# Experts stage of a mixture-of-experts block: a fifth product bank, silu on ScalarE, a quarter of the low parts on GpSimd, and an earlier turn of the gated rows

## The chip, the cores and the metric

The kernel runs on one core of one Trainium2 chip. A core has TensorE (PE: matmuls and the weight loads ahead of them), VectorE (DVE), ScalarE (ACT), GpSimd (POOL) and SyncE (SP), which run their own instruction streams and meet through semaphores, and 16 DMA engines. SBUF is the on-chip memory of 128 partitions; PSUM has eight banks into which PE writes its products. The metric is the device time of one launch in microseconds (us), lower is better.

## What is computed

Two blocks in a row on 2048 tokens of width 1024, all float32: a hybrid mixer block, then (after an embedding norm that puts 16 meta tokens in front) attention of two kinds and a mixture of 32 experts with the four best of them for each token. The change is in the experts. Their part of the reference:

```python
def _clamped_swiglu(hgu):
    x_glu = jnp.minimum(hgu[..., ::2], SWIGLU_LIMIT)
    x_lin = jnp.clip(hgu[..., 1::2], -SWIGLU_LIMIT, SWIGLU_LIMIT)
    return x_glu * jax.nn.sigmoid(SWIGLU_ALPHA * x_glu) * (x_lin + 1.0)
...
    xs = h[tok]
    hgu = lax.ragged_dot(xs, w_gate_up, group_sizes) + b_gate_up[e_sorted]
    act = _clamped_swiglu(hgu)
    out = lax.ragged_dot(act, w_down, group_sizes) + b_down[e_sorted]
```

SWIGLU_LIMIT is 7, SWIGLU_ALPHA 1.702, w_gate_up is 32 x 1024 x 2048 and w_down 32 x 1024 x 1024.

## The kernel before

Seven stages follow each other: mixer, join, project, attend, route, experts, combine. The route stage sorts the rows by expert and writes tables (`R.tab`, and `tabd` with the row numbers). The experts stage, from about 3101 to 6178 us, is a loop over 32 groups; a group is an expert with up to 512 rows, that is r = 1 to 4 row blocks of 128. Each engine runs its own copy of that loop (experts_sync, experts_pool, experts_pe, experts_act, experts_dve) with its own order written out by hand; blocks b >= r are skipped by branches on values read from the table. Nothing else sets the order.

A group has six phases c, one for each slab of 512 columns: c = 0 to 3 are gate and up, c = 4 and 5 are down. For each slab SP loads 2 MB into `raw[c % 2]` (two phases ahead). To keep float32 precision each product is made of three: weights and rows are split into a high part (fp32r) and a low part. ACT casts the slab's four pieces of 128x1024 to `wh` (`high`, L2354), DVE subtracts them from raw into `wl` (`lows`, L2407), in phase c for the slab of c+1. When all four low pieces are done, DVE gives `raw` back to SP (`raw_free`). PE (`product`, L2311) then makes, for each row block b, 24 matmuls of 128x512 into one PSUM bank, `product_bank(c, b) = (b + 2c) % 4`; it takes `g_free` of the bank first. For b = 0 it takes `w_full` before k = 0, 2, 4, 6, one for each low piece.

DVE empties a bank in one of two ways. `gated` (c < 4, L2441 to L2447) adds the bias (`e_tt`), clamps gate (`e_gg`) and up (`e_uu`), waits for ACT's sigmoid (`e_sg`, L2386) and multiplies them into `e_act`. `outcome` (c = 4, 5, L2453) adds the bias into `e_Y`, which ACT stores to `yd`.

In between come transposes of PE, which are called turns here. `acts(c-1, b)` (L2294) turns the gated rows of the last phase into bank 6 or 7 (`TA`), ACT takes their high part (L2340), DVE the low part (`e_aTl`, L2407). `rows(b)` (L2286) turns the next group's gathered rows in banks 4 and 5 (`TX`), a half in each, in c = 4 at k = 4; blocks that the present group hasn't got are turned in c = 5 at k = 6. `between` says where in a product each stands: `acts` after two of eight k (after four for b = 0, except in c = 4). POOL's loop loads the row numbers (`e_idx`) of the group and gathers its row blocks into the two buffers of `hx` (L2269), each by an indirect DMA whose landing it waits for. `settle` is a 1x1 memset with a wait for it, `link` a wait for the instruction itself, `take` a wait on a semaphore that is then counted down.

The trace puts every wait of the stage down to L2204, the line of `take`.

## Time and profile before

| | us |
|---|---|
| median of three runs | 6391.53 (6390.81 to 6391.83) |
| profiled execution, whole | 6390.21 |
| its span | 6389.1 |
| experts stage in it | 3101 to 6178 |

| engine | busy us | share of the span |
|---|---|---|
| PE matmul | 5677.8 | 89% |
| PE weight load (beside matmuls) | 4489.7 | 70% |
| DVE | 3814.2 | 60% |
| ACT | 2232.1 | 35% |
| POOL | 749.0 | 12% |

Busy times are of the whole span. The record of a matmul lasts longer than the distance to the next one, since they are pipelined; distances are read from starts. An idle time in square brackets stands before the instruction that ended it, with what released it. A window is named by its two ends in us from the span's start. The DMA queue of SP lands a slab of 2 MB in 8.0 to 8.4 us in the middle.

### The profile page before, as it was taken

To read this page: it belongs to the slowest core of one execution; us is meant where nothing else is said; L and a number is where in the kernel's file an instruction comes from. 1 tells how busy PE (TensorE), PEld (TensorE's weight loads), DVE (VectorE), ACT (ScalarE), POOL (GpSimd) and SP (SyncE) were. 2 spreads that over 40 slices of the span, in tenths; PEclk is the share of its full clock that TensorE was granted. 3 is DMA by queue.
4 is the path that set the end of the run, shared out by engine and by line. 5 is a ranking of instruction groups with operands and counts; after the bars stand their busy time and mean duration, and the time that the engine had idled before them with its cause. 6 is when DMAs were issued, how large, how long until landed. Compare 5 with 4: busy or idle time off the path is not lost. (4 is left out here: it accounts for less than half of the span.)

```text
span 6389.1 us, 82690 instructions
## 1 busy us (share of the span) xinstructions
PE 5677.8 (89%) x26393; PEld 4489.7 (70%) x26394; DVE 3814.2 (60%) x7593; ACT 2232.1 (35%) x4436; POOL 749.0 (12%) x566
## 2 busy tenths in 40 slices
PE   8999896997999999979699999999998999988960
PEld 7777675775777777757577777777776877766740
DVE  6676574223555666657556556556566555666658
ACT  3444412333333344433233233333344232444421
POOL 1111053221000000025200000000000000000016
PEclk9999998998999999989799999999999999999985
DMA  3333333446210010033244444435455343565557
GB/s 134 116 115 104 112 125 111 126 126 212 85 44 35 28 41 22 9 113 105 86 167 160 147 159 171 158 135 200 175 206 208 127 154 142 201 224 217 204 191 259
DMA packets 278153, 871.47 MB, mean 136 GB/s; under 512 B 22304, under 2 KB 167312, under 8 KB 235664
## 3 DMA queue, kind: packets, MB, share of 16 engines
q1 hardware_dynamic: 228256, 744.21, 33.0%
q0 software_dynamic: 24576, 77.83, 3.8%
q10 hardware_dynamic: 24944, 45.37, 1.9%
q8 instruction: 119, 1.95, 0.1%
q14 instruction: 258, 2.11, 0.1%
HBM read 723.15 MB, written 144.18 MB: 136 GB/s over the span
## 5 line engine op out<-in xcount | busy, mean ns | idle before, releaser
L2407 DVE TENSOR_TENSOR e_wl<-r_raw,e_wh 128x1024 fp32r<-128x1024 f32 x772 | 908.7, 1221 | 344.6 <-DVEq L2204 344.6
L2311 PE MATMUL ps<-e_wh,e_hTh 128*128 128x512 f32 x2496 | 1026.0, 411 | 67.8 <-PEq L2204 67.8
L2311 PE MATMUL ps<-e_wh,e_hTl 128*128 128x512 f32 x2496 | 1002.7, 402 | 0.0
L2311 PE MATMUL ps<-e_wl,e_hTh 128*128 128x512 f32 x2496 | 1001.5, 401 | 0.0
L2354 ACT CAST e_wh<-r_raw 128x1024 fp32r<-128x1024 f32 x772 | 769.2, 1049 | 193.7 <-ACTq L2204 186.5
L2311 PEld LDWEIGHTS ps<-e_wh,e_hTh 128*128 128x128 f32 x2496 | 479.9, 192 | 187.7 <-issue 84.5
L2311 PE MATMUL ps<-e_wh,e_aTh 128*128 128x512 f32 x1248 | 513.6, 412 | 58.6 <-PEq L2204 58.6
L2311 PEld LDWEIGHTS ps<-e_wh,e_hTl 128*128 128x128 f32 x2496 | 478.4, 192 | 115.8
L2311 PEld LDWEIGHTS ps<-e_wl,e_hTh 128*128 128x128 f32 x2496 | 480.2, 192 | 104.3
L2386 ACT ACTIVATE e_sg<-e_gg 128x256 f32<-128x256 f32 x312 | 130.7, 419 | 1205.4 <-ACTq L2204 1205.4
L1614 PE MATMUL ps<-a_PT,a_V 128*128 128x512 f32 (+1 forms) x1088 | 548.9, 596 | 0.7 <-ACT a_oT L1670 0.7
L1683 DVE TENSOR_REDUCE a_sc<-ps 128x1 f32<-128x416 f32 (+1 forms) x640 | 365.2, 588 | 257.4 <-PE ps L1592 257.4
L2311 PE MATMUL ps<-e_wh,e_aTl 128*128 128x512 f32 x1248 | 496.2, 398 | 0.0
L2311 PE MATMUL ps<-e_wl,e_aTh 128*128 128x512 f32 x1248 | 495.7, 397 | 0.0
L1592 PE MATMUL ps<-a_K,a_Q 128*128 128x416 f32 (+1 forms) x1920 | 456.3, 367 | 21.3 <-DMA a_KR<-kTd 18.2
L1592 PEld LDWEIGHTS ps<-a_K,a_Q 128*128 128x128 f32 x1920 | 356.4, 189 | 77.4 <-issue 70.7
L2441 DVE TENSOR_TENSOR e_tt<-ps,e_bg 128x512 f32<-128x512 f32 x312 | 215.4, 690 | 310.1 <-DVEq L2204 309.5
L2269 POOL DMA_INDIRECT e_hx<-h1d,e_idx x78 | 89.4, 1146 | 2493.2 <-POOLq L2204 2301.9
L1600 PEld LDWEIGHTS ps<-ident,a_P 128*128 128x128 f32 (+1 forms) x2176 | 258.5, 138 | 170.5 <-issue 131.2
L1663 ACT ACTIVATE a_P<-ps,a_sc 128x416 f32<-128x416 f32 (+1 forms) x640 | 378.1, 606 | 0.0
L380 PE MATMUL ps<-m_xh,m_wh 128*128 128x512 f32 x896 | 353.8, 395 | 5.3 <-DVE m_wl L665 5.3
L1697 DVE COPY a_PT<-ps 128x512 f32<-128x512 f32 x384 | 265.2, 692 | 152.1 <-PE ps L1600 152.1
(358 smaller groups left out, 9547.3 us busy)
## 6 DMA issues: line engine op xcount, KB each, us to landing
r_raw<-in_wgu SPq DMA_DIRECT2D x130, 2048.0 KB, 8.4
r_raw<-in_wdn SPq DMA_DIRECT2D x64, 2048.0 KB, 8.0
m_raw<-in_w SPq DMA_DIRECT2D x56, 1024.0 KB, 4.9
yd<-e_Y ACTq DMA_DIRECT2D x156, 256.0 KB, 7.6
e_bg<-in_bgu SPq DMA_DIRECT2D x32, 1024.0 KB, 10.8
qTd<-p_qt SPq DMA_DIRECT2D x32, 640.0 KB, 5.9
yd<-a_zt SPq DMA_DIRECT2D x32, 512.0 KB, 6.7
e_bd<-in_bdn SPq DMA_DIRECT2D x32, 512.0 KB, 8.9
```

Source lines behind the costliest of these rows:

```text
L380: t = pe.matmul(p[:, :], x[:, w, i, j * 128:(j + 1) * 128], y[:, c % 2, i, :], start=(n == 0), stop=(n == 23))
L1592: t = pe.matmul(p[:, 0:w], x, y, start=(n == 0), stop=(n == len(todo) - 1))
L1600: t = pe.transpose(p[0:n, k * 128:(k + 1) * 128], P.P[:, m % 2, c * 512 + k * 128:c * 512 + k * 128 + n], ident[:])
L1614: t = pe.matmul(ps[b][:, :], P.V[0:r, n % 2, j, :], P.PT[0:r, G % 2, j, :], start=(j == 0), stop=(j == NT - 1))
L1663: act.activation(P.P[:, m % 2, lo:lo + w], p[:, 0:w], ACT.Exp, bias=P.sc[:, m % 2, 6:7], scale=scale, accum_out=P.sc[:, m % 2, 8 + c:9 + c ...
L1683: dve.tensor_reduce(z[:, c:c + 1], p[:, 0:SCW[c][1]], AX, ALU.max).then_inc(*v.step("max", m, c))
L1697: dve.tensor_copy(P.PT[:, G % 2, 4 * c:4 * c + 4, q], p[:, :].rearrange("p (k q) -> p k q", k=4)).then_inc(*v.step("t", n, c))
L2311: t = pe.matmul(E.G[g][:, :], x[:, b, k, :], y[:, c % 2, k, :], start=(n == 0), stop=(n == 23))
L2354: act.copy(E.wh[:, n % 2, 2 * i:2 * i + 2, :].rearrange("p k n -> p (k n)"), E.raw[:, n % 2, 2 * i:2 * i + 2, :].rearrange("p k n -> p (k ...
L2386: act.activation(E.sg[:], E.gg[:], ACT.Sigmoid, scale=1.702).then_inc(E.sig, 1)
L2407: return dve.tensor_tensor(lo, src, hi.bitcast(F32), ALU.subtract)
L2441: dve.tensor_tensor(E.tt[:], E.G[g][:, :], E.bg[:, c * 512:(c + 1) * 512], ALU.add).then_inc(E.g_free[g], 1)
```

## The change

1. `product_bank` gives bank b, but bank 4 for b = 0 in odd phases. Banks 5 to 7 (`T`) turn both kinds of rows: `acts(b)` in 5 or 6, `rows(b)` its first half in 7 and its second half in the one of 5 and 6 that `acts(b)` doesn't use; that half shares the semaphore `a_free`.
2. ACT computes silu with scale 1.702 in place of sigmoid, so that gate times sigmoid is 1/1.702 of it; the product of `e_uu` and `e_gg` on DVE goes, and `outcome` multiplies by 1/1.702 as it adds the bias. `e_tt` is waited for with `link` instead of `settle`.
3. The third of the four low pieces of each slab is made by GpSimd (`low` in experts_pool); PE takes `w_pool` for it, and SP needs two releases of `raw`.
4. `acts(3, b)` in c = 4 is turned before the product's first matmul.
5. POOL fetches the next group's row numbers and rows during the present group, with its six low pieces between them: low 1, low 2, gathers 0 and 1, low 3, 4, 5, gathers 2 and 3, low 0 of the next group.
6. Row block 0 is no longer under a branch (`present`). The combine stage reuses semaphores of earlier stages.

```diff
-    E.G, E.TX, E.TA = banks.ap[0:4], banks.ap[4:6], banks.ap[6:8]
+    E.G, E.T = banks.ap[0:5], banks.ap[5:8]
...
 def product_bank(c, b):
-    return (b + 2 * c) % 4
+
+    return b if b or c % 2 == 0 else 4
+
+
+def turn_bank(E, b, hf):
+
+    return E.T[2] if hf == 0 else E.T[(b + 1) % 2]
+
+
+def present(eng, r, b):
+
+    return eng.If(r > b) if b else nullcontext()
+
+
+
+POOL_PART = 2
...
-    if k == (2 if b or c == 4 else 4) and 1 <= c <= 4:
+    if k == (0 if c == 4 else 2 if b else 4) and 1 <= c <= 4:
...
-        take(sp, E.raw_free[c % 2])
+        take(sp, E.raw_free[c % 2], 2)
...
 def experts_pool(nc, E):
     pool = nc.gpsimd
-    with groups(E, pool) as q:
-        r = entry(E, pool, 1, q, 1, 4)
+
+    def places(q):
+
         row = entry(E, pool, 2, q, 0, NE * CAP - 512)
-        blk = entry(E, pool, 3, q, 0, YB)
         pool.dma_start(E.idx[:], E.tabd[bass.ds(row, 512), :].rearrange("(j p) o -> p (j o)", p=128),
                        allow_slow_non_contiguous=True).then_inc(E.idx_full, 16)
-        pool.wait_ge(E.idx_full, q * 16 + 16)
-        for b in range(4):
-            with pool.If(r > b):
-                take(pool, E.hx_free[b % 2])
-                pool.indirect_dma_start(out=E.hx[:, b % 2, :], out_offset=None, in_=E.h1d,
-                                        in_offset=bass.IndirectOffsetOnAxis(ap=E.idx[:, b:b + 1], axis=0)).then_inc(E.rows_in, 16)
-                pool.wait_ge(E.rows_in, blk * 16 + (16 * b + 16))
-                pool.sem_inc(E.hx_full[b % 2], 1)
+
+    def gather(r, blk, b):
+        with pool.If(r > b):
+            take(pool, E.hx_free[b % 2])
+            pool.indirect_dma_start(out=E.hx[:, b % 2, :], out_offset=None, in_=E.h1d,
+                                    in_offset=bass.IndirectOffsetOnAxis(ap=E.idx[:, b:b + 1], axis=0)).then_inc(E.rows_in, 16)
+            pool.wait_ge(E.rows_in, blk * 16 + (16 * b + 16))
+            pool.sem_inc(E.hx_full[b % 2], 1)
+
+    def low(n):
+
+        ks = slice(2 * POOL_PART, 2 * POOL_PART + 2)
+        take(pool, E.hi_pool)
+        pool.tensor_tensor(E.wl[:, n % 2, ks, :].rearrange("p k n -> p (k n)"),
+                           E.raw[:, n % 2, ks, :].rearrange("p k n -> p (k n)"),
+                           E.wh[:, n % 2, ks, :].rearrange("p k n -> p (k n)").bitcast(F32), ALU.subtract).then_inc(E.pl, 1)
+        take(pool, E.pl)
+        pool.sem_inc(E.w_pool, 1)
+        pool.sem_inc(E.raw_free[n % 2], 1)
+
+    places(0)
+    first, blk = entry(E, pool, 1, 0, 1, 4), entry(E, pool, 3, 0, 0, 4 * GT)
+    pool.wait_ge(E.idx_full, 16)
+    for b in range(4):
+        if b == 2:
+            low(0)
+        gather(first, blk, b)
+    with groups(E, pool) as q:
+        places(q + 1)
+        low(1)
+        rn = entry(E, pool, 1, q + 1, 0, 4)
+        blkn = entry(E, pool, 3, q + 1, 0, 4 * GT)
+        pool.wait_ge(E.idx_full, q * 16 + 32)
+        low(2)
+        gather(rn, blkn, 0)
+        gather(rn, blkn, 1)
+        for n in (3, 4, 5):
+            low(n)
+        gather(rn, blkn, 2)
+        gather(rn, blkn, 3)
+        low(0)
...
-            take(pe, E.x_free[hf])
+            take(pe, E.x_free if hf == 0 else E.a_free[(b + 1) % 2])
             for k in range(4):
-                t = pe.transpose(E.TX[hf][:, k * 128:(k + 1) * 128],
+                t = pe.transpose(turn_bank(E, b, hf)[:, k * 128:(k + 1) * 128],
                                  E.hx[:, b % 2, (4 * hf + k) * 128:(4 * hf + k + 1) * 128], ident[:])
             t.then_inc(E.x_full[hf], 1)
...
-                take(pe, E.w_full)
+                take(pe, E.w_pool if k == 2 * POOL_PART else E.w_full)
...
-                     E.raw[:, n % 2, 2 * i:2 * i + 2, :].rearrange("p k n -> p (k n)")).then_inc(E.hi_full, 1)
+                     E.raw[:, n % 2, 2 * i:2 * i + 2, :].rearrange("p k n -> p (k n)")).then_inc(E.hi_pool if i == POOL_PART else E.hi_full, 1)
...
-                        between(act, c, b, r, rn, acts, rows, 2)
-                        between(act, c, b, r, rn, acts, rows, 4)
+                        for k in (0, 2, 4):
+                            between(act, c, b, r, rn, acts, rows, k)
                     if c < 4:
                         take(act, E.glu)
-                        act.activation(E.sg[:], E.gg[:], ACT.Sigmoid, scale=1.702).then_inc(E.sig, 1)
+                        act.activation(E.sg[:], E.gg[:], ACT.Silu, scale=SWIGLU_ALPHA).then_inc(E.sig, 1)
...
+            if i == POOL_PART:
+                continue
...
-        dve.tensor_tensor(E.tt[:], E.G[g][:, :], E.bg[:, c * 512:(c + 1) * 512], ALU.add).then_inc(E.g_free[g], 1)
-        settle(3)
+        link(dve.tensor_tensor(E.tt[:], E.G[g][:, :], E.bg[:, c * 512:(c + 1) * 512], ALU.add))
+        dve.sem_inc(E.g_free[g], 1)
         dve.tensor_scalar(E.gg[:], E.tt[:, 0:256], 7.0, None, ALU.min).then_inc(E.glu, 1)
         link(dve.tensor_scalar(E.uu[:], E.tt[:, 256:512], 7.0, -7.0, ALU.min, ALU.max))
-        link(dve.scalar_tensor_tensor(out=E.uu[:], in0=E.uu[:], scalar=1.0, in1=E.gg[:], op0=ALU.add, op1=ALU.mult))
         take(dve, E.sig)
-        dve.tensor_tensor(E.act[:, b, :], E.uu[:], E.sg[:], ALU.mult).then_inc(E.act_full[b], 1)
+        dve.scalar_tensor_tensor(out=E.act[:, b, :], in0=E.uu[:], scalar=1.0, in1=E.sg[:], op0=ALU.add, op1=ALU.mult).then_inc(E.act_full[b], 1)
 
     def outcome(c, b):
         g = product_bank(c, b)
         take(dve, E.g_full[g])
         take(dve, E.out_free[b], 16)
-        dve.tensor_tensor(E.Y[:, b, :], E.G[g][:, :], E.bd[:, (c - 4) * 512:(c - 3) * 512], ALU.add).then_inc(E.out_full[b], 1)
+        dve.scalar_tensor_tensor(out=E.Y[:, b, :], in0=E.G[g][:, :], scalar=1.0 / SWIGLU_ALPHA, in1=E.bd[:, (c - 4) * 512:(c - 3) * 512],
+                                 op0=ALU.mult, op1=ALU.add).then_inc(E.out_full[b], 1)
```

The same renamings (`E.T`, `turn_bank`, `present`, the third place k = 0 in the loops of b > 0) are in experts_act and experts_dve, and ACT's warm-up at the loop's start names Silu.

DVE from the end of a group's first phase to the first product of the second, before: `e_wl` are low pieces of slab 2, `ps` are banks.

```order
L2407 TENSOR_TENSOR e_wl<-r_raw,e_wh 128x1024 x2
L2407 TENSOR_TENSOR e_aTl<-ps6,e_aTh 128x256
L2407 TENSOR_TENSOR e_wl<-r_raw,e_wh 128x1024 x2
L2404 MEMSET e_junk 1x1
L2441 TENSOR_TENSOR e_tt<-ps2,e_bg 128x512
L2404 MEMSET e_junk 1x1
L2443 TENSOR_SCALAR e_gg<-e_tt 128x256
L2444 TENSOR_SCALAR e_uu<-e_tt 128x256
L2445 SCALAR_TENSOR_TENSOR e_uu<-e_uu,e_gg 128x256
L2447 TENSOR_TENSOR e_act<-e_uu,e_sg 128x256
```

DVE at the same place now:

```order
L2462 TENSOR_TENSOR e_wl<-r_raw,e_wh 128x1024 x2
L2462 TENSOR_TENSOR e_aTl<-ps5,e_aTh 128x256
L2462 TENSOR_TENSOR e_wl<-r_raw,e_wh 128x1024
L2459 MEMSET e_junk 1x1
L2498 TENSOR_TENSOR e_tt<-ps4,e_bg 128x512
L2500 TENSOR_SCALAR e_gg<-e_tt 128x256
L2501 TENSOR_SCALAR e_uu<-e_tt 128x256
L2503 SCALAR_TENSOR_TENSOR e_act<-e_uu,e_sg 128x256
```

Of the four low pieces the third has gone, and each gated product has two instructions fewer; its first one reads bank 4 where it was bank 2.

PE in the down product of b = 0, c = 4, from its start to the end of the turns, before: `e_act` are gated rows, `e_hx` the next group's rows.

```order
L2311 MATMUL ps0<-e_wl,e_aTh 128x512
L2311 MATMUL ps0<-e_wh,e_aTl 128x512
L2294 MATMUL ps6<-ident,e_act 128x128 x2
L2311 MATMUL ps0<-e_wh,e_aTh 128x512
L2311 MATMUL ps0<-e_wl,e_aTh 128x512
L2311 MATMUL ps0<-e_wh,e_aTl 128x512
L2311 MATMUL ps0<-e_wh,e_aTh 128x512
L2311 MATMUL ps0<-e_wl,e_aTh 128x512
L2311 MATMUL ps0<-e_wh,e_aTl 128x512
L2225 COMPARE_AND_BRANCH
L2286 MATMUL ps4<-ident,e_hx 128x128 x4
L2286 MATMUL ps5<-ident,e_hx 128x128 x4
```

PE at the same place now:

```order
L2349 MATMUL ps5<-ident,e_act 128x128 x2
L2366 MATMUL ps0<-e_wh,e_aTh 128x512
L2366 MATMUL ps0<-e_wl,e_aTh 128x512
L2366 MATMUL ps0<-e_wh,e_aTl 128x512
L2366 MATMUL ps0<-e_wh,e_aTh 128x512
L2366 MATMUL ps0<-e_wl,e_aTh 128x512
L2366 MATMUL ps0<-e_wh,e_aTl 128x512
L2366 MATMUL ps0<-e_wh,e_aTh 128x512
```

and, two matmuls further on:

```order
L2366 MATMUL ps0<-e_wh,e_aTh 128x512
L2366 MATMUL ps0<-e_wl,e_aTh 128x512
L2366 MATMUL ps0<-e_wh,e_aTl 128x512
L2247 COMPARE_AND_BRANCH
L2341 MATMUL ps7<-ident,e_hx 128x128 x4
L2341 MATMUL ps6<-ident,e_hx 128x128 x4
```

The turn of the gated rows has moved ahead of the first matmul, and the second half of the next group's rows goes to a bank, 6, that gated rows use too.

POOL's loop over the groups before, from the row numbers to the second gather (the other two follow in the same way):

```order
L2263 DMA e_idx<-tabd 128x4x1
L2265 ISA
L2269 DMA e_hx<-h1d,e_idx 128x1024
L2271 ISA
L2267 UNCONDITIONAL_BRANCH
L2267 COMPARE_AND_BRANCH
L2269 DMA e_hx<-h1d,e_idx 128x1024
L2271 REGISTER_ALU
```

POOL's loop now, from its second low piece, that of slab 2, to those of slabs 3 to 5:

```order
L2300 TENSOR_TENSOR e_wl<-r_raw,e_wh 128x1024
L2289 COMPARE_AND_BRANCH
L2291 DMA e_hx<-h1d,e_idx 128x1024
L2293 ISA
L2289 UNCONDITIONAL_BRANCH
L2289 COMPARE_AND_BRANCH
L2291 DMA e_hx<-h1d,e_idx 128x1024
L2293 ISA
L2289 UNCONDITIONAL_BRANCH
L2300 TENSOR_TENSOR e_wl<-r_raw,e_wh 128x1024 x3
```

The gathers now fetch for the next group; the low pieces 3 to 5 stand behind two of them.

## Rows read from the trace of the kernel before

**Rows 1.** Windows view, experts stage: core, busy us (instructions) by engine, PEclk, DMA, GB/s
```profile
3101.00:6178.00 3077.00, 2839.73 (x12480) 2261.23 (x12480) 1856.91 (x3915) 1095.27 (x1616) 114.91 (x111) 0.97 0.48 174
```

**Rows 2.** Timeline of PE, 3787.5:3790.2: start us, us, engine line, op [idle before, releaser]
```profile
3787.73 0.40 PE L2311 MATMUL ps<-e_wl,e_aTh 128*128 128x512 f32 x1
3787.96 0.40 PE L2311 MATMUL ps<-e_wh,e_aTl 128*128 128x512 f32 x1
3789.78 0.47 PE L2311 MATMUL ps<-e_wh,e_aTh 128*128 128x512 f32 x1 [1.43 <-PEq L2204]
```

**Rows 3.** Waits of PE, 3101:6178: engine, line, waited for: us in total, times, longest
```profile
PE ps L2311 <- PEq L2204: 126.4, 98, 4.6
PE ps L2294 <- PEq L2204: 70.2, 30, 4.4
```

**Rows 4.** Waits of PE in 3577:3809, in 3881:4349 and in 4498:4619, a row each
```profile
PE ps L2311 <- PEq L2204: 15.1, 12, 1.4
...
PE ps L2311 <- PEq L2204: 33.7, 24, 4.6
...
PE ps L2311 <- PEq L2204: 10.5, 6, 4.1
```

**Rows 5.** Timeline of DVE, 3785:3790.2, the down products' bank being emptied
```profile
3788.62 0.69 DVE L2453 TENSOR_TENSOR e_Y<-ps,e_bd 128x512 f32<-128x512 f32 x1 [3.41 <-DVEq L2204]
```

**Rows 6.** Timeline of PE, at 5881 and at 5921
```profile
5881.33 0.41 PE L2294 MATMUL ps<-ident,e_act 128*128 128x128 f32 x2 [3.56 <-PEq L2204]
...
5921.21 0.47 PE L2311 MATMUL ps<-e_wh,e_aTh 128*128 128x512 f32 x1 [0.80 <-PEq L2204]
```

**Rows 7.** Timeline of DVE, loop-back at 4006, group at 5862 to 5920
```profile
4006.76 2.36 DVE L2407 TENSOR_TENSOR e_wl<-r_raw,e_wh 128x1024 fp32r<-128x1024 f32 x2 [3.35 <-DVEq L2204]
...
5871.85 4.63 DVE L2407 TENSOR_TENSOR e_wl<-r_raw,e_wh 128x1024 fp32r<-128x1024 f32 x4 [6.30 <-DVEq L2204]
...
5878.42 0.69 DVE L2441 TENSOR_TENSOR e_tt<-ps,e_bg 128x512 f32<-128x512 f32 x1 [1.93 <-DVEq L2204]
...
5880.95 0.69 DVE L2441 TENSOR_TENSOR e_tt<-ps,e_bg 128x512 f32<-128x512 f32 x1
...
5914.67 0.43 DVE L2447 TENSOR_TENSOR e_act<-e_uu,e_sg 128x256 f32<-128x256 f32 x1 [0.26 <-DVEq L2204]
```

**Rows 8.** Waits of PE in a group of one row block, 5720:5779
```profile
PE ps L2294 <- PEq L2204: 10.1, 4, 3.9
```

**Rows 9.** Page, costliest groups: line engine op xcount, busy us, mean ns, idle
```profile
L2407 DVE TENSOR_TENSOR e_wl<-r_raw,e_wh 128x1024 fp32r<-128x1024 f32 x772 | 908.7, 1221 | 344.6 <-DVEq L2204 344.6
```

**Rows 10.** Timeline of GpSimd, 3054:3058
```profile
3054.95 2.39 POOL L2135 TENSOR_TENSOR o_h<-o_h,o_LN 128x1024 f32<-128x1024 f32 x1 [4.92 <-DVE o_h L2029]
```

**Rows 11.** Timeline of DVE, 3043:3060, the same line twice
```profile
3043.67 0.19 DVE L2034 TENSOR_TENSOR o_Macc<-o_Macc,o_M 128x32 f32<-128x32 f32 x1
...
3055.00 2.40 DVE L2034 TENSOR_TENSOR o_Macc<-o_Macc,o_M 128x32 f32<-128x32 f32 x1
```

**Rows 12.** Timelines of DVE and of GpSimd, 1114:1117
```profile
1114.69 0.69 DVE L1323 TENSOR_TENSOR p_kt<-ps,p_kt 128x512 fp32r<-128x512 f32 x1 [4.49 <-ACT p_kt L1297]
...
1114.67 1.81 POOL L1426 TENSOR_TENSOR p_ra<-p_ra,p_rp 128x768 f32<-128x768 f32 x1
```

**Rows 13.** Tile e_hx on GpSimd: instruction; landings of all, of 3433:3449, 5931:5933, 5923:5926
```profile
L2269 POOL DMA_INDIRECT e_hx<-h1d,e_idx x78: 934/971/1577, 3106.6 to 6010.2; - x78
...
DMA to landing us min/median/max: 4.1/5.1/10.6
...
DMA to landing us min/median/max: 4.2/6.7/9.2
...
DMA to landing us min/median/max: 8.9/8.9/8.9
...
DMA to landing us min/median/max: 4.8/4.8/4.8
```

**Rows 14.** Timeline of GpSimd, 72:82
```profile
73.17 7.38 POOL L800 TENSOR_TENSOR m_tmp<-m_Ct 128x526 f32<-128x526 f32 x1 [70.19 <-ACT m_Ct L552]
```

63 lines of the change are left out of this document (33 added, 30 removed).

## The prediction

> **What bounds the kernel now.** The page's shares say PE 89% busy, but that is a mean over seven stages. The change lies in the experts stage, so I read that stretch alone: 3101 to 6178 us, 3077 of the 6389.1 us [rows 1]. PE runs 12480 instructions there; 1248 are transposes (78 row blocks with eight for their rows and eight for their gated rows), 11232 are 512-column matmuls. In an undisturbed run they start 0.233 us apart (3787.73 and 3787.96 in [rows 2]), so they need 11232 x 0.2333 = 2620 us. The granted clock of the stretch is 0.97 [rows 1]. PE is the bound, and what can be won is its waits. The largest are 126.4 ahead of products and 70.2 ahead of gated rows' turns [rows 3]; DVE and ACT are busy 1857 and 1095 of 3077 us, so neither sets the pace over the whole, though either may in one group.
>
> The waits have three forms. The run of matmuls between two group starts tells how many row blocks each of the 32 groups has: 3 groups have one, 17 two, 7 three, 5 four (78 together). Call them r=1 to r=4.
> (a) r=3. The third product of a phase and the first of the next share a bank, since (2+2c)%4 = (2(c+1)+0)%4, so PE must wait until DVE has emptied what it has just finished. The three stretches that hold the seven r=3 groups show 12 + 24 + 6 = 42 waits, six in a group, 59.3 us [rows 4]. One in detail: the matmul after 3787.96 starts at 3789.78, 1.82 us later where 0.233 is normal, so it costs 1.59 while the profile counts 1.43 idle [rows 2]; DVE's emptying starts at 3788.62 and takes 0.69 [rows 5], and DVE had been idle for 3.41 before it, so nothing else was late.
> (b) r=2. PE waits 3.56 at 5881.33 to turn the first gated rows, and 0.80 at 5921.21 in the down product for the low part of the last ones [rows 6]. The first comes from DVE's loop-back: it does nothing for 6.30 us before 5871.85; in another group this is 3.35 [rows 7].
> (c) r=1. PE waits 10.1 us for gated rows in one group of 59 us [rows 8]: here DVE is the bound.
>
> **The change, part by part.** The sum is made against the profiled execution, 6390.21 us (span 6389.1); the median of the runs is 6391.53, 1.3 more.
>
> *1. Fifth bank.* In odd phases the first product goes to bank 4, so banks of neighbouring products are never shared at r=3 (c5's third product uses bank 2, the next group's first bank 0). All 42 waits go: 59.3 + 42 x 0.16 (the 1.59 - 1.43 above) = -66 us. What is late next at r=3? DVE's phase is three gated products at most 2.53 apart, four low pieces of 1.22 and three small ones, near 14 us, in 17.4 us of PE: nothing.
>
> *2. Gated rows of c=3 turned ahead of c=4's first matmul instead of after 6.* Their low part is then ready by matmul 18, and both 0.80 waits of an r=2 group go (with their 0.16: 1.9 us; in some groups over 3, I take 2.35). But the turn now needs act(3,0) at the start. PE gets there at 5921.21 - 0.97 - 18 x 0.233 - ten transposes (1.1) = 5914.9, act(3,0) ends at 5914.67 + 0.43 = 5915.1 [rows 7]; with a low piece that is late by 0.9 (part 4) PE waits 1.2, and another 0.55 where rows(0) and acts share a bank. Net 0.6 per group, 17 groups: -10 us. Bounds: -40 (nothing is given back) and +10 (both waits a microsecond longer).
>
> *3. Shared turning bank.* rows(b) uses the bank of acts(b+1) for its second half, so the second turn of c=4 waits for it, by the order 0.75 us at most: 7 r=3 groups +5, 5 r=4 groups -3 (they lose the 1.3 of the old place): +2. Bounds 0 and +9.
>
> *4. Silu and the low pieces.* The first e_tt to the next takes 5880.95 - 5878.42 = 2.53 us [rows 7]. One product of 0.42 and its link go, the silu can't start before gg and act not before silu, so about 0.34 goes: 2.19. Of four low pieces (1.22 each [rows 9], 1.15 apart) the third goes to GpSimd. What does it cost there? A 128x1024 tensor_tensor took 2.39 on it [rows 10]. The point is what DVE does in those 2.39 us. A 128x32 sum of two SBUF tiles takes 0.19 at 3043.67; at 3055.00, beside GpSimd's op, it takes 2.40 and ends with it [rows 10, 11]. An op with one PSUM input takes its 0.69 beside a GpSimd op of 1.81 at 1114.67 [rows 12]. DVE's fourth low piece has two SBUF inputs, so it starts only when GpSimd's is done: low pieces at 0 and 1.15, GpSimd to 2.3 + 2.4 + its wake-up, fourth 1.22: 6.2 instead of 4.9. So DVE does not win 1.2 per slab, it loses about 1.25 where nothing stands between (0.9 with aTl between, 0.4 with settle), less 0.34 for each gated product. Phases c=1 to 3 at r=2: DVE needs 11.95 us where PE takes 11.62 (48 matmuls and four transposes). It falls 0.33 behind per phase, and the turn of the gated rows has 2.4 us of slack ahead of PE, so PE stays the bound: no cost. At r=3 and 4 there is more room. The first-phase wait (b): 14 r=2 groups with the long loop-back win 0.34 each, the three with the short one lose 1: -5 + 3 = -2. The extreme that DVE is not held at all (it then saves 1.15 per slab) is rival B; that GpSimd's op is longer is D.
>
> *5. r=1 groups.* DVE is the bound. Turn at the start +1.4, held low pieces less the 0.34 +1.5, and low piece 3 stands behind two gathers on Pool's queue, whose lateness moves the release of raw and with it a slab load, +2.6: +5.5 x 3 = +16. Bounds +3 and +45 (rival C).
>
> *6. Pool's queue.* Pool waits for each gather to land, and behind it stand low(3), low(4), low(5); the last gathers stand before low(0). Landing: min 4.1, median 5.1, max 10.6; the long ones are issued beside a slab load (5931.5: 8.9; 5924.8: 4.8), and a pair at 3433:3449 took 4.2 + 9.2 [rows 13]. At r=2 two landings of 4.2 to 9.2 and GpSimd's piece behind them end 11.5 to 15 us after low(2), and PE wants low(3) a phase and a half after low(2), 1.5 x 11.62 = 17.4: hidden. Ahead of the first group low(0) stands between gathers: +3. gather 2 and 3 after low(5), beside the group's loop-back: +7 (5 r=4 and 7 r=3 groups, about 0.6 each). Bounds 0 and +20 for the two.
>
> Sum: -66 - 10 + 2 - 2 + 16 + 3 + 7 = -50. 6390.2 - 50 = 6340.2, and with the 1.3: 6341.
>
> The gather instruction itself takes 934 to 1577 ns, 971 in the middle, with DVE ops going on beside it all the time [rows 13]. The Trainium skill ("SBUF — State Buffer", section "SBUF: two separate sides") says that a GpSimd-issued DMA of about 620 ns takes about 3100 ns beside a DVE copy, since its descriptors wait for the shared port. The rows do not show a wait of that size. Were it so in the new order, each gather would cost about 2.5 us more: low(3) would end 19 us after low(2), 1.5 us late in 14 r=2 groups (+21) and the r=1 groups +15, an estimate from that page that would give about 6377.
>
> **Rivals.**
> *B. The port does not bite.* If DVE's low piece runs through GpSimd's, DVE wins 1.15 per slab. Then the c=4 turn gives nothing back (-34 for part 2) and the 14 + 3 waits for the first gated rows shrink by 1.2 to 1.5 (-21); with -66, +2, +3 and +8 for r=1 and +3 for Pool, -105: 6286. For it: PSUM reads are not held [rows 12]. Against: every pair of two-SBUF-input ops in [rows 10, 11].
> *C. Slower: gathers in front of low(3).* If in most groups the two landings sum to more than about 14 us (they would be issued beside slab loads), low(3) ends 24 us after low(2) (10 + 10 + the piece and the waits), 6.5 us after PE wants it: 14 x 6.5 = +91, r=1 3 x 15 = +45, less the 16 that part 5 has: +120 on the forecast, 6461. For it: 8.9 and 9.2 beside loads. Against: the pair's sum of 13.4, and the median of 5.1 [rows 13].
> *D. DVE becomes the bound at r=2.* GpSimd's wait for the port works both ways: its first op at 73.17 took 7.38 beside a full DVE [rows 14]. If each low piece took 0.85 us more, DVE would need 12.8 for 11.62: 1.2 x 4 phases x 17 = 82, less the slack of 2.4 x 17 = 41. Between 6381 and 6422, middle 6402.
> *E. It gives back at r=3 what it takes.* The matmuls come 1.6 us earlier and meet DVE's low pieces late: 6390. Against: DVE idle 3.41 before 3788.62 [rows 5].
>
> **How the numbers follow.** Forecast 0.62, with its own range 6315 to 6365 (parts 2, 5 and 6 by their bounds); B 0.15; C 0.07; D 0.08, about a third of it slower; E 0.04; the estimate by the page 0.04, half of it faster. A measurement of this kernel can tell 0.2% (13 us) from no change. Faster: 0.62 + 0.15 + 0.02 and a little of D = 0.80; slower: 0.07 + 0.03 = 0.10; within 0.2%: 0.10. The range must take in B's centre, since B and C together are more than 0.2, and the lower half of D: 6280 to 6395.
>
> **What would show it.** Waits of PE in 3577:3809 near nothing, and r=3 groups six times 1.57 = 9.4 us shorter. GpSimd's low pieces near 2.4 us with DVE's fourth held beside them, as 3.6 us in the record in place of 1.22. The e_tt to e_tt distance 2.2. In r=2 groups a wait ahead of the first turn of c=4 and none at matmul 18. Pool's low(3) ends before PE's c=3. Wrong would be: PE waits at the third quarter of a slab (low pieces late), landings over 7 us in both gathers, or r=1 groups longer by 15.

## The result

| | before, us | changed, us |
|---|---|---|
| median (five runs each) | 6391.83 (6390.81 to 6395.58) | 6418.62 (6410.22 to 6423.45) |
| profiled execution | 6390.21 | 6410.22 |
| its span | 6389.1 | 6409.1 |
| experts stage, first to last matmul | 3041.9 | 3064.9 |

The changed kernel is slower: the ratio is 1.004 (95% interval 1.0025 to 1.0055). It takes 6418.6 us where 6341 was forecast. The profiled execution is the fastest of the five, 8 us under their median, so the 20 us between the two profiled executions are a little less than the 27 us between the medians. The experts stage is 23 us longer, its start has moved forward by 1.7, and what lies behind it is 1.4 shorter.

### The profile page after: what moved, and what is told of

The parts are those of the page before. It is cut to its first block and busy times, and to the rows that moved or that the text cites. A ratio compares the mean times of both kernels' runs of the same rounds, so it can differ in the third digit from the quotient of the medians.

```text
span 6409.1 us, 82692 instructions
## 1 busy us (share of the span) xinstructions
PE 5683.6 (89%) x26393; PEld 4502.2 (70%) x26394; DVE 3705.5 (58%) x6776; ACT 2229.0 (35%) x4436; POOL 1225.7 (19%) x760
## 5 line engine op out<-in xcount | busy, mean ns | idle before, releaser
L2462 DVE TENSOR_TENSOR e_wl<-r_raw,e_wh 128x1024 fp32r<-128x1024 f32 x579 | 896.7, 1578 | 389.5 <-DVEq L2209 384.9
L2366 PE MATMUL ps<-e_wh,e_hTh 128*128 128x512 f32 x2496 | 1025.6, 411 | 31.9 <-PEq L2209 31.9
L2366 PE MATMUL ps<-e_wh,e_hTl 128*128 128x512 f32 x2496 | 1002.0, 401 | 0.0
L2366 PE MATMUL ps<-e_wl,e_hTh 128*128 128x512 f32 x2496 | 1002.0, 401 | 0.0
L2300 POOL TENSOR_TENSOR e_wl<-r_raw,e_wh 128x1024 fp32r<-128x1024 f32 x193 | 489.3, 2535 | 2072.6 <-POOLq L2209 2072.6
L2366 PEld LDWEIGHTS ps<-e_wh,e_hTh 128*128 128x128 f32 x2496 | 481.0, 193 | 142.0 <-issue 37.2
L2366 PEld LDWEIGHTS ps<-e_wh,e_hTl 128*128 128x128 f32 x2496 | 478.8, 192 | 116.1
L2366 PEld LDWEIGHTS ps<-e_wl,e_hTh 128*128 128x128 f32 x2496 | 480.9, 193 | 105.5
L2366 PE MATMUL ps<-e_wh,e_aTh 128*128 128x512 f32 x1248 | 513.8, 412 | 2.2 <-PEq L2209 2.1
L2366 PE MATMUL ps<-e_wl,e_aTh 128*128 128x512 f32 x1248 | 499.2, 400 | 0.0
L2366 PE MATMUL ps<-e_wh,e_aTl 128*128 128x512 f32 x1248 | 499.1, 400 | 0.0
```

Source lines behind the costliest of these rows:

```text
L2300: pool.tensor_tensor(E.wl[:, n % 2, ks, :].rearrange("p k n -> p (k n)"), E.raw[:, n % 2, ks, :].rearrange("p k n -> p (k n)"), E.wh[:, n ...
L2366: t = pe.matmul(E.G[g][:, :], x[:, b, k, :], y[:, c % 2, k, :], start=(n == 0), stop=(n == 23))
L2462: return dve.tensor_tensor(lo, src, hi.bitcast(F32), ALU.subtract)
```

## The profile after

The page's part 1 for PE, and two groups of its part 5: line, engine, operation, shapes, count, busy us, mean ns, idle time before.

```profile
PE 5683.6 (89%) x26393; PEld 4502.2 (70%) x26394; DVE 3705.5 (58%) x6776; ACT 2229.0 (35%) x4436; POOL 1225.7 (19%) x760
...
L2462 DVE TENSOR_TENSOR e_wl<-r_raw,e_wh 128x1024 fp32r<-128x1024 f32 x579 | 896.7, 1578 | 389.5 <-DVEq L2209 384.9
...
L2300 POOL TENSOR_TENSOR e_wl<-r_raw,e_wh 128x1024 fp32r<-128x1024 f32 x193 | 489.3, 2535 | 2072.6 <-POOLq L2209 2072.6
```

The first answer to the change stands in the second line. DVE makes 579 low pieces where it made 772 [rows 9], a quarter less, and is busy with them for 896.7 us where it was 908.7: the mean has gone from 1221 to 1578 ns. GpSimd spends 489.3 us on its 193. So 193 pieces were handed over and 12 us of DVE's time came back.

The waits of PE in the experts stage (3132:6198): engine, line, what it waited for, us in total, times, longest. L2349 turns gated rows, L2341 the next group's rows, L2366 is the product.

```profile
PE ps L2349 <- PEq L2209: 147.2, 77, 8.7
PE ps L2341 <- PEq L2209: 47.0, 14, 3.9
PE ps L2366 <- PEq L2209: 34.0, 16, 4.8
```

Against [rows 3] the product's waits fell from 126.4 (98 times) to 34.0 (16 times): those of the bank are gone. Those ahead of the gated rows doubled, 70.2 to 147.2. For b = 0 in c = 1 to 3 a product's wait for GpSimd's low piece is counted here too, since it comes just before the turn at k = 4.

The windows view of the same stretch, columns as in [rows 1]:

```profile
3132.00:6198.00 3066.00, 2837.50 (x12448) 2267.70 (x12448) 1738.97 (x3083) 1085.60 (x1605) 584.04 (x299) 0.97 0.48 173
```

The same stretch of the kernel before, from its first to its last product:

```profile
3134.00:6176.00 3042.00, 2831.72 (x12448) 2254.95 (x12448) 1846.79 (x3898) 1087.34 (x1605) 110.30 (x106) 0.98 0.48 175
```

DVE's busy time fell from 1847 to 1739 us, and PE waited longer all the same. The mean length of a group, from its first matmul to the next group's, read from the timeline of PE, says where:

| kernel | stage | r=1 (3) | r=2 (17) | r=3 (7) | r=4 (5) |
|---|---|---|---|---|---|
| before | 3041.9 | 57.0 | 79.4 | 116.1 | 141.8 |
| changed | 3064.9 | 66.2 | 81.5 | 109.3 | 143.1 |

The r=3 groups gave 48 us, the r=1 groups took 28, the r=2 groups 36 and the r=4 groups 6.

In 13 of the 17 r=2 groups a new wait stands at the same place, c = 3 at k = 4, where PE wants the piece that GpSimd made of slab 3 and then turns gated rows. In the three r=1 groups PE waited 2.7 us there before, too, for gated rows; now it waits 6.8 to 8.7. One of the new waits on PE, and GpSimd's timeline ahead of it:

```profile
5471.86 0.66 PE L2349 MATMUL ps<-ident,e_act 128*128 128x128 f32 x2 [2.73 <-PEq L2209]
```

```profile
5450.57 2.46 POOL L2300 TENSOR_TENSOR e_wl<-r_raw,e_wh 128x1024 fp32r<-128x1024 f32 x1 [10.68 <-POOLq L2209]
5454.16 0.99 POOL L2291 DMA_INDIRECT e_hx<-h1d,e_idx  x1 [1.13 <-POOLq L2209]
5464.48 0.93 POOL L2291 DMA_INDIRECT e_hx<-h1d,e_idx  x1 [9.32 <-POOLq L2209]
5468.93 2.35 POOL L2300 TENSOR_TENSOR e_wl<-r_raw,e_wh 128x1024 fp32r<-128x1024 f32 x1 [3.52 <-POOLq L2209]
```

The landings of the gathers (min/median/max) in the whole kernel, of the first of these two and of the second, and the load of the next slab on SP:

```profile
DMA to landing us min/median/max: 4.0/9.1/11.5
...
DMA to landing us min/median/max: 9.4/9.4/9.4
...
DMA to landing us min/median/max: 4.2/4.2/4.2
```

```profile
5454.51 0.33 SPq L2261 DMA_DIRECT2D r_raw<-in_wdn  x1
```

GpSimd ends low(2) at 5453.03, issues gather 0 at 5454.16 (9.4 to landing), gather 1 at 5464.48 (4.2), starts low(3) at 5468.93 and ends at 5471.28; PE goes on at 5471.86. From low(2) to low(3) it is 18.2 us. The sixteen waits make 53 us, 1.3 to 3.5 in an r=2 group and 7 to 9 in an r=1 group, of which 8 us were there before. The load at 5454.51 is no accident: SP waits for two releases of `raw`, one from GpSimd at the end of low(2), the other from DVE behind its fourth piece, which ends 1.1 us later since it was held. So the end of low(2) lets the gather go and, by way of DVE, a 2 MB load: the two issues are 0.34 to 0.54 us apart in 30 of the 31 groups. Before, GpSimd had nothing but the gathers in its queue; the first of a pair went out 2.2 us ahead of a load in most groups, and the middle landing was 5.1 us [rows 13]; now it is 9.1.

What DVE did beside GpSimd's two low pieces:

```profile
5451.50 2.61 DVE L2462 TENSOR_TENSOR e_wl<-r_raw,e_wh 128x1024 fp32r<-128x1024 f32 x1 [0.42 <-DVEq L2209]
...
5469.32 2.24 DVE L2503 SCALAR_TENSOR_TENSOR e_act<-e_uu,e_sg 128x256 f32<-128x256 f32 x1 [0.48 <-DVEq L2209]
5471.49 2.35 DVE L2462 TENSOR_TENSOR e_wl<-r_raw,e_wh 128x1024 fp32r<-128x1024 f32 x2
```

The piece at 5451.50 takes 2.61 where 1.22 is normal, and ends 1.1 after GpSimd's; e_act at 5469.32, two inputs in SBUF, takes 2.24 for 0.43 and delays DVE's next pieces to 5471.49. This is called the hold below: DVE's instruction does not get done until GpSimd's has ended. It is so without exception: 159 of DVE's 579 pieces start inside one of GpSimd's, and each ends 1.08 or 1.09 us after it.

The gathers behind low(5) are late too. In an r=3 group GpSimd's last low piece of the group, gather 2 behind it, and PE's wait for these rows:

```profile
4080.09 2.37 POOL L2300 TENSOR_TENSOR e_wl<-r_raw,e_wh 128x1024 fp32r<-128x1024 f32 x1 [16.04 <-POOLq L2209]
4083.56 0.95 POOL L2291 DMA_INDIRECT e_hx<-h1d,e_idx  x1 [1.10 <-POOLq L2209]
...
4094.52 1.06 PE L2341 MATMUL ps<-ident,e_hx 128*128 128x128 f32 x8 [3.35 <-PEq L2209]
```

That is 3.35 us, and six groups with r = 3 or 4 have it, 3.3 to 3.8 each. Ahead of the first group the second to fourth turn wait 17.4 us in place of 10.7, but the first one comes after 10.90 idle in place of 17.98, so the prologue as a whole costs nothing; it lies ahead of the stage as measured here.

Such a wait has a price behind it that no wait shows. After the 3.35 us the matmuls start 0.43 us apart where 0.23 is normal, and the granted clock is 0.50, the lower of its two levels (1.2 and 2.4 GHz). PE, and the windows view of two stretches:

```profile
4096.36 0.63 PE L2366 MATMUL ps<-e_wh,e_aTh 128*128 128x512 f32 x1
4096.78 0.63 PE L2366 MATMUL ps<-e_wl,e_aTh 128*128 128x512 f32 x1
...
4096.00:4099.00 3.00, 3.00 (x9) 2.33 (x8) 1.28 (x3) 0.33 (x1) 0.00 (x0) 0.50 0.46 175
4101.00:4104.00 3.00, 3.00 (x15) 2.41 (x14) 0.96 (x1) 2.15 (x3) 0.00 (x0) 1.00 0.23 87
```

In the experts stage 208 matmuls start so late before and 245 in the changed kernel, 40 and 47 us more than at the upper level. Of the 29 stretches at the lower level before, 26 follow a wait of 2.6 to 4.9 us. So this is not what made the change slower, but it adds to what long waits cost.

An r=1 group, 5733:5800, to be held against [rows 8]:

```profile
PE ps L2349 <- PEq L2209: 17.0, 4, 8.7
PE ps L2366 <- PEq L2209: 4.8, 1, 4.8
```

## The experiments

The experts stage starts between 3129 and 3161 us in these profiles, also on the same chip, though of what stands ahead of it only GpSimd's part for the first group was edited; behind it there are 211 to 213 us in each. So each profile is also read by the length of that stage, from one execution of each kernel. Ratios are to the kernel before on the same chip; the chips differ between some of the kernels. The kernel that ran twice, on two chips, differs by 2.4 us of stage. A length of a stage is compared with the 3041.9 of the kernel before, which has one profile.

| kernel | median | ratio (95%) | stage | r=1 | r=2 | r=3 | r=4 |
|---|---|---|---|---|---|---|---|
| bank alone | 6338.2 | 0.9919 (0.9903 to 0.9936) | 2979.5 | 56.5 | 79.5 | 107.0 | 141.9 |
| the same again | 6338.2 | 0.9911 (0.9894 to 0.9927) | 2981.9 | 56.4 | 79.6 | 107.0 | 142.0 |
| bank, silu | 6353.1 | 0.9921 (0.9904 to 0.9937) | 2990.1 | 57.4 | 80.1 | 106.8 | 141.7 |
| bank, early turn | 6354.1 | 0.9921 (0.9905 to 0.9938) | 2995.7 | 58.7 | 79.9 | 107.2 | 142.1 |
| bank, turn at k=1 | 6349.7 | 0.9913 (0.9897 to 0.9930) | 2990.4 | 57.8 | 79.9 | 107.0 | 141.9 |
| changed without GpSimd's share | 6345.2 | 0.9930 (0.9914 to 0.9947) | 2993.8 | 60.2 | 79.8 | 106.8 | 141.7 |
| changed, queue free | 6344.4 | 0.9929 (0.9913 to 0.9946) | 3002.1 | 61.4 | 80.3 | 106.5 | 141.5 |
| changed, gathers spread | 6369.5 | 0.9957 (0.9941 to 0.9974) | 3017.6 | 62.6 | 80.8 | 106.5 | 142.3 |
| changed, gathers behind low(3) | 6415.7 | 1.0018 (1.0008 to 1.0027) | 3055.4 | 64.1 | 81.1 | 109.6 | 143.4 |
| changed, fourth piece on GpSimd | 6411.8 | 1.0034 (1.0024 to 1.0044) | 3060.2 | 65.6 | 80.4 | 110.4 | 144.6 |
| bank, branches nested | 6325.7 | 0.9892 (0.9876 to 0.9909) | 2968.4 | 54.1 | 79.3 | 107.0 | 141.9 |
| the same with a free share | 6341.2 | 0.9919 (0.9902 to 0.9935) | 3001.3 | 59.5 | 80.8 | 106.1 | 141.4 |

### The bank alone

Everything but the first part of the change undone (and row block 0 left without its branch):

```diff
-                i == POOL_PART: continue        (DVE makes four pieces, GpSimd's loop as before)
-    k == (0 if c == 4 else 2 if b else 4)
+    k == (2 if b or c == 4 else 4)
-    ACT.Silu
+    ACT.Sigmoid, and gated() and outcome() as before
```

> Only the fifth bank (with the three banks for turning that it forces) is left; sigmoid, DVE's four low pieces, the old GpSimd loop and the late turn of the gated rows are as in the kernel before. Theory (the bank is worth what the prediction said, and the loss of the change comes from other parts): the 42 waits at r=3 go, about 10 us for each of the 7 groups, r=2 groups stay near 79 us; 6391.8 - 66 + 5 = about 6331. Rival (the stall moves to another wait, so the bank brings little): r=3 groups stay above 113 us, 6375 to 6392.

Measured: 6338.2, ratio 0.9919 (52 us), and 2979.5 for the stage, 62.4 less than before. The waits of PE in it (L2333 the product, L2316 the gated rows):

```profile
PE ps L2333 <- PEq L2209: 76.3, 70, 3.5
PE ps L2316 <- PEq L2209: 72.1, 36, 5.1
```

The product's waits fell from 126.4 to 76.3 us, and the r=3 groups by 9.1 us each; those ahead of gated rows hardly moved from 70.2. By the stage the bank is worth what the prediction said, and nothing gave it back. The rival falls.

### Without GpSimd's share

```diff
-            if i == POOL_PART:
-                continue
-                take(pe, E.w_pool if k == 2 * POOL_PART else E.w_full)
+                take(pe, E.w_full)
-        take(sp, E.raw_free[c % 2], 2)
+        take(sp, E.raw_free[c % 2])
...
 def experts_pool: the loop of the kernel before
```

> The changed kernel without GpSimd's share: DVE makes all four low pieces, GpSimd's loop is the old one; fifth bank, silu and early turn stay. Theory (GpSimd's share costs the time: gathers in front of its low pieces, and DVE held beside them): the waits for a turn at c=3, k=4 (16 of 3.3 us) and the late rows of c=4 and 5 go, r=1 groups return to 57 us or less, r=2 to about 78, r=3 to 106; 6300 to 6320. Rival (silu or the early turn costs it): the time stays at 6390 to 6420.

Measured: 6345.2, stage 2993.8. Waits of PE (L2316 gated rows, L2333 the product):

```profile
PE ps L2316 <- PEq L2209: 114.3, 63, 5.8
PE ps L2333 <- PEq L2209: 34.7, 17, 4.8
```

71 us of stage time hang on GpSimd's share, that is its low pieces and the queue order that they came with. But it was 25 us slower than the 6320 that the theory allowed at most, and 12 to 14 us of stage behind the bank alone: silu and the early turn don't pay either, which the theory had left out.

### The queue or the hold: gathers that are not waited for

```diff
         low(2)
-        gather(rn, blkn, 0)
-        gather(rn, blkn, 1)
-        for n in (3, 4, 5):
-            low(n)
-        gather(rn, blkn, 2)
-        gather(rn, blkn, 3)
-        low(0)
+        gather(rn, 0)
+        gather(rn, 1)
+        low(3)
+        landed(rn, blkn, 0)
+        low(4)
+        gather(rn, 2)
+        low(5)
+        landed(rn, blkn, 2)
+        gather(rn, 3)
+        landed(rn, blkn, 3)
+        low(0)
```

`gather` issues and `landed` waits and tells PE; `landed(rn, blkn, 0)` waits for gathers 0 and 1. The order ahead of the first group is changed in the same way.

> The changed kernel with GpSimd's low pieces kept, but its queue no longer waits for the first two landings ahead of low(3), and gather 2 stands ahead of low(5). Theory Q (the queue behind the gathers is most of the loss): 16 waits of 3.3 us at c=3, k=4 and most waits for rows in c=4 and 5 (49 us in all) go, 6310 to 6335, close to the kernel without GpSimd's share. Rival P (DVE held beside GpSimd's op is most of it): the gain over the changed kernel is under 30 us, 6390 or more, and the c=3 waits turn into waits for low pieces or gated rows of the same length.

Measured: 6344.4, stage 3002.1. The waits (L2365 gated rows, L2382 the product), and DVE's low pieces:

```profile
PE ps L2365 <- PEq L2209: 127.5, 64, 4.5
PE ps L2382 <- PEq L2209: 32.8, 17, 4.8
```

```profile
L2478 DVE TENSOR_TENSOR e_wl<-r_raw,e_wh 128x1024 fp32r<-128x1024 f32 x579 | 923.9, 1625 | 398.5 <-DVEq L2209 397.8
```

The landings are as late as in the changed kernel (median 9.2), DVE's pieces are held as much (923.9 us in all), and the time is that of the kernel without the share, 9 us over the most that theory Q gave. So 63 us of stage are the queue: pieces and row turns behind landings. Of the waits at c = 3, k = 4 those of the r=2 groups are gone, and the three of the r=1 groups are back at 2.0 to 3.3 us. The hold shows as another wait: up to 2.7 us ahead of the turn at the start of c = 4 in the r=2 groups, 43 us in all, where the changed kernel has 5 and the kernel without the share has 5. The share with a free queue costs 0 by the medians and 8 us by the stage.

### The fourth piece instead of the third

```diff
-POOL_PART = 2
+POOL_PART = 3
```

> The changed kernel with the fourth low piece on GpSimd instead of the third, all else the same. DVE then has three low pieces in a row and meets GpSimd's op with its next e_tt (one input in PSUM) instead of with a low piece. If an operand in PSUM spares DVE the wait and the hold matters: the low pieces' mean falls from 1.58 to near 1.22 us; but the clamps and e_act that follow are held instead where they fall in the 2.4 us. If the queue is what costs (theory Q): low(3) is wanted by PE a quarter later (k=6), so the 16 waits shrink by 1.4 us each, about -25 us, 6390 to 6400. If the hold is what costs (rival P): -60 us or more.

Measured: 6411.8, stage 3060.2, 5 us better than the changed kernel. DVE's low pieces and its clamp of the gate:

```profile
L2462 DVE TENSOR_TENSOR e_wl<-r_raw,e_wh 128x1024 fp32r<-128x1024 f32 x579 | 794.4, 1409 | 336.5 <-DVEq L2209 336.5
L2500 DVE TENSOR_SCALAR e_gg<-e_tt 128x256 f32<-128x256 f32 x312 | 150.1, 481 | 75.4 <-DVEq L2209 75.4
```

The pieces fell to 1409 only, and e_gg rose from 325 ns to 481: what escapes the hold as a low piece meets it as a clamp. Two gathers still stand ahead of low(3). The r=2 groups' waits at c = 3 fell from 28 to 4 us, as theory Q had said, but 15 came back ahead of the turns and at matmul 18 of c = 4, and the r=3 and r=4 groups grew by 1.1 and 1.5 us each. So both theories promised too much: 5 us of stage came in place of 25, and the hold theory (60 us) falls clearly.

### One gather ahead of a piece instead of two

```diff
-        low(2)
+        pool.sem_inc(E.pl, 1)
+        take(pool, E.pl)
         gather(rn, blkn, 0)
+        low(2)
         gather(rn, blkn, 1)
-        for n in (3, 4, 5):
-            low(n)
+        low(3)
+        low(4)
         gather(rn, blkn, 2)
+        low(5)
         gather(rn, blkn, 3)
         low(0)
```

> The changed kernel with the same gathers, each still waited for, and the same low pieces on GpSimd, but never two gathers in a row: gather 0 ahead of low(2), gather 1 ahead of low(3), gather 2 ahead of low(5), gather 3 ahead of low(0). Theory (two landings in a row are what makes low(3) late; one of 9 us and the piece fit in the 17.4 us): the 16 waits at c=3, k=4 and those for rows(2) go, experts stage 3000 to 3015 against 3065, whole about 6345 to 6360. Rival (any gather beside a slab load ahead of a piece is too much): the waits come back at c=2 and c=3, 3050 or more.

Measured: 6369.5, stage 3017.6, a little over the 6360 and 3015 that the theory allowed, and far from its rival. GpSimd in an r=2 group, and the landings of all gathers:

```profile
5410.71 0.99 POOL L2291 DMA_INDIRECT e_hx<-h1d,e_idx  x1 [2.66 <-POOLq L2209]
5420.22 2.92 POOL L2300 TENSOR_TENSOR e_wl<-r_raw,e_wh 128x1024 fp32r<-128x1024 f32 x1 [8.51 <-POOLq L2209]
5424.25 0.97 POOL L2291 DMA_INDIRECT e_hx<-h1d,e_idx  x1 [1.11 <-POOLq L2209]
5432.86 2.42 POOL L2300 TENSOR_TENSOR e_wl<-r_raw,e_wh 128x1024 fp32r<-128x1024 f32 x1 [7.64 <-POOLq L2209]
...
DMA to landing us min/median/max: 4.1/9.3/11.0
```

The same gathers, each waited for, each as slow as before (9.3 in the middle), with the same pieces: low(2) to low(3) is now 12.1 us (5423.14 to 5435.28), inside PE's 17.4, and the waits at c = 3, k = 4 went from 53 to 9 us, about what the r=1 groups had before the change (8). 47 us of stage by the order alone. The 15 us that are left against the free queue lie in r=2 groups (8), r=1 groups (4) and r=4 groups (4). A part of them is gathers 2 and 3 of groups that grow: 7.5 to 7.7 us before a fourfold group, where the free queue has 5.9 to 6.4.

### The same pair one piece later

```diff
-        low(2)
+        for n in (2, 3):
+            low(n)
         gather(rn, blkn, 0)
         gather(rn, blkn, 1)
-        for n in (3, 4, 5):
+        for n in (4, 5):
             low(n)
```

> The changed kernel with one thing moved: gathers 0 and 1 stand behind low(3) instead of ahead of it, each still waited for. If what hurts is that a low piece stands behind two landings of about 14 us, the waits at c=3, k=4 go and come back at c=4, k=4 ahead of low(4) (3 us in r=2 groups): within 15 us of the changed kernel, 6405 to 6425. If it is the place beside the slab load at low(3) alone: 6360 to 6370.

Measured: 6415.7, inside what the first theory gave, stage 3055.4. GpSimd from low(3) on, and PE at c = 4, k = 4:

```profile
5473.52 2.44 POOL L2300 TENSOR_TENSOR e_wl<-r_raw,e_wh 128x1024 fp32r<-128x1024 f32 x1 [9.29 <-POOLq L2209]
5477.09 0.99 POOL L2291 DMA_INDIRECT e_hx<-h1d,e_idx  x1 [1.13 <-POOLq L2209]
5487.35 0.93 POOL L2291 DMA_INDIRECT e_hx<-h1d,e_idx  x1 [9.27 <-POOLq L2209]
5491.80 2.49 POOL L2300 TENSOR_TENSOR e_wl<-r_raw,e_wh 128x1024 fp32r<-128x1024 f32 x1 [3.51 <-POOLq L2209]
...
5494.98 1.07 PE L2342 MATMUL ps<-ident,e_hx 128*128 128x128 f32 x8 [1.38 <-PEq L2209]
```

The stall goes along with the pair: low(4) ends at 5494.29, 18.3 us after low(3), and PE, which wanted it, goes on at 5494.98. It is smaller there (1.4 here, 0.7 to 1.9 in 13 r=2 groups); PE had already waited up to 2.0 for gated rows at the start of c = 4 in ten of them, so this comes off it.

### Silu, and the early turn, each alone with the bank

Silu with the turn as before (it brings with it the `link` behind e_tt in place of `settle`, and the 1/1.702 in `outcome`); and the early turn with sigmoid. Both against the changed kernel:

```diff
 bank_silu:
-    k == (0 if c == 4 else 2 if b else 4)
+    k == (2 if b or c == 4 else 4)
 bank_turn:
-    ACT.Silu
+    ACT.Sigmoid, and gated() and outcome() as before
```

> Fifth bank and silu; GpSimd's share, its new loop and the early turn are undone. It stands between the kernel with the bank alone (experts stage 2980 us) and the one without GpSimd's share (2994). If silu is what makes those 14 us (its e_act comes later after e_gg, so the first gated rows of r=2 groups are turned later): 2990 or more. If it saves the 0.34 for each gated product of the prediction: 2970 to 2978.

Measured: 6353.1, stage 2990.1, 8 to 11 more than the bank alone. DVE in the changed kernel, the first two gated products of a group:

```profile
5442.89 0.69 DVE L2498 TENSOR_TENSOR e_tt<-ps,e_bg 128x512 f32<-128x512 f32 x1 [1.91 <-DVEq L2209]
...
5444.97 0.43 DVE L2503 SCALAR_TENSOR_TENSOR e_act<-e_uu,e_sg 128x256 f32<-128x256 f32 x1 [0.64 <-DVEq L2209]
5445.31 0.68 DVE L2498 TENSOR_TENSOR e_tt<-ps,e_bg 128x512 f32<-128x512 f32 x1
```

From the first e_tt to the next it is 2.42 us, where it was 2.53 [rows 7]: 0.11 saved, not 0.34. The product that went had filled a part of the time in which DVE waits for ACT: 0.64 ahead of e_act. That holds for the first gated product of a group; from the second to the third, at r = 3 and 4, it is 2.25 for 2.53, so 0.28 saved. In the kernel with bank and silu the first product is even slower, 2.62 to 2.65 in 28 of the 29 groups that have a second one:

```profile
5399.04 0.69 DVE L2463 TENSOR_TENSOR e_tt<-ps,e_bg 128x512 f32<-128x512 f32 x1 [1.93 <-DVEq L2209]
5400.37 0.29 DVE L2465 TENSOR_SCALAR e_gg<-e_tt 128x256 f32<-128x256 f32 x1 [0.64 <-DVEq L2209]
```

Here DVE idles 0.64 ahead of e_gg, where the others have 0.24. Where the 8 to 11 us come from can be seen, why it is so cannot: DVE's idle time between its last instruction of a group and the first low piece of the next is 6.65 and 4.01 us in the mean (after r=1 or 2, and after r=3 or 4), where the bank alone has 6.17 and 3.55, and the waits ahead of the first gated rows grew by 12 us. The kernel without GpSimd's share has the same (6.81 and 4.02), the changed kernel, with silu too, has not (6.17 and 3.54). So silu alone does not decide it. The pauses stand at fixed places of DVE's loop and differ from kernel to kernel; what makes them is not shown.

> Fifth bank and the early turn of c=4; sigmoid, no share of GpSimd. If the early turn makes the 14 us (at r=1 PE waits 4.4 to 6.0 us for act(3,0) ahead of the product, where it waited 2.8 to 4.1 after six matmuls): experts stage 2990 or more, the loss in the three r=1 groups. If it brings the 10 us of the prediction's part 2: 2970.

Measured: 6354.1, stage 2995.7, 14 to 16 more. The r=1 groups grew by 2.3 us each, 7 in all. In the others the waits at matmul 18 went, 57 us, and 47 us came back ahead of the second turn of c = 4 and 17 ahead of the first (1.6 to 1.8 in a group). So the 10 us that the prediction expected are not there.

### A turn between the two places

PE turns after three matmuls, ACT and DVE take the rows before their first piece:

```diff
-def between(eng, c, b, r, rn, acts, rows, k):
+def between(eng, c, b, r, rn, acts, rows, k, turn=0):
-    if k == (2 if b or c == 4 else 4) and 1 <= c <= 4:
+    if k == (turn if c == 4 else 2 if b else 4) and 1 <= c <= 4:
-            between(pe, c, b, r, rn, acts, rows, k)
+            between(pe, c, b, r, rn, acts, rows, k, 1)
```

> Fifth bank, sigmoid, no share of GpSimd, and the gated rows of c=4 turned after three matmuls (k=1) on PE, with ACT and DVE taking them ahead of their low and high pieces. If the waits at matmul 18 (0.4 to 1.9, and 0.9, in nearly every group) come from ACT and DVE taking the turned rows late, and the cost of the early turn from PE standing at the product's start: both go, 1.5 us for each r=2 group and 1.0 for each r=3 and r=4 group, experts stage 2945 to 2955, whole 6300 to 6312. Rival (the shared bank and act(3,0) are late all the same): 2975 to 2990.

Measured: 6349.7, stage 2990.4 (the profiled execution is 13 us over the median; its stage starts at 3160, later than any other). In every group of r=3 and 4 a wait of 0.9 stands before the second turn and one of 0.4 at matmul 18, where it was 0.4 and 0.9 at matmul 18 of the first and of the second product; at r=2 it is mostly 1.5 and 0.5 against 1.0 and 0.9. The sum stays, the rival holds (its upper end was 2990). What it suggests is that DVE frees the bank and takes the rows in a chain of its own, and PE can choose only where it stands waiting.

### Nested branches

```diff
-            for b in range(4):
-                with present(dve, r, b):
+            with ExitStack() as deep:
+                for b in range(4):
+                    if b:
+                        deep.enter_context(dve.If(r > b))
```

(the same on PE and ACT)

> The kernel with the fifth bank alone, with the branches of the absent row blocks nested, so that an engine at r=2 or r=1 leaves a phase by one jump instead of two or three. It asks where DVE's 3.6 or 6 to 7 us between two groups come from: they are 3.6 after groups with r=3 or 4 and 6 or more after r=2 and 1. If the jumps over absent blocks make them, they shrink to near 4 everywhere, the waits of 3.6 us for the first gated rows go in 14 groups, experts stage 2930 to 2945. Rival (it is the DMA traffic beside the fetch of instructions): no change, 2975 to 2985.

Measured: 6325.7, stage 2968.4, 13 less than the same kernel unnested on the same chip, but not in the way expected. DVE's pause between groups is what it was: 3.27 to 3.65 after the 12 groups with r = 3 or 4, 4.69 to 7.20 after the 19 others (3.27 to 3.70 and 4.60 to 7.20 in the same kernel unnested); the jumps don't make it. The 13 us are in r=1 groups (54.1 for 56.4, 7 us) and in r=2 groups, there mostly in the waits at c = 4. At 2968 it lies between the theory (2945 at most) and the rival (2975 at least), so neither fits.

> The kernel with the fifth bank alone once more, on the same chip as its nested form: experts stage 2980, ratio to the kernel before 0.992, if its lead over the kernels with silu or with the early turn (2990 to 2996) is more than the spread between chips; 2990 or more if it is not.

Measured: 2981.9, ratio 0.9911: the lead over silu and early turn holds by stage (8 to 14 us), though the ratios of the whole overlap.

### The share once more, on the fastest form

```diff
+ bank_nest with low pieces on GpSimd, w_pool, hi_pool and the queue of gathers_free
```

> The fastest form so far (fifth bank, nested branches, sigmoid, late turn) with GpSimd's low pieces and the queue that does not wait between gathers and pieces. If DVE is held beside GpSimd's op for as long as it saves, the share is worth nothing even with a free queue: experts stage 2968 to 2980, ratio 0.989 to 0.991, DVE's pieces at 1.6 us each and 900 us in all. Rival (the share pays once the queue is free): stage 2960 or less, ratio under 0.987.

Measured: 6341.2, ratio 0.9919, stage 3001.3, so neither: with a free queue the share costs 15 us by the medians (other chips) and 33 by the stage. DVE's low pieces:

```profile
L2488 DVE TENSOR_TENSOR e_wl<-r_raw,e_wh 128x1024 fp32r<-128x1024 f32 x579 | 914.1, 1605 | 383.5 <-DVEq L2209 382.6
```

914 us for 579 pieces. The r=1 groups grew by 5.4 us each, the r=2 groups by 1.5. One reading is that the hold is no longer covered where DVE's chain ends the waits. But DVE's pauses at fixed places grew as well: from the first e_tt to the next it is 2.92 us in the middle where the kernel without the share has 2.53, and after r = 1 or 2 it idles 6.90 between groups in the mean, for 6.16. No run takes the hold or these pauses away alone, so how the 33 us divide is open.

## Why the prediction was wrong

The time left the range on the slow side (6418.6 against 6395 at most), by the mechanism of rival C, which had 0.07. Of the signs that the prediction named for being wrong, PE's waits at the third quarter of a slab came; of the two landings only the first is over 7 us, and the r=1 groups grew by 9, not 15.

- **What bounds it** was right: PE's waits, in the three forms.
- **Part 1, the bank, -66** (with part 3, -64): right by the stage. Alone it gave 62.4 and 60.0 us of it, and 52 to 57 us of the whole.
- **Part 6, GpSimd's queue, +10**: this step failed. The queue was priced at 10 us as hidden behind PE's work; it cost 63 us of stage, from the changed kernel to its free queue (3064.9 to 3002.1). Three things were wrong in it. First, "two landings of 4.2 to 9.2 and GpSimd's piece behind them end 11.5 to 15 us after low(2)" left out what lies between them: 1.13 to the first issue, 0.95 from landing to the second issue, 0.27 to the piece. With 9.4 + 4.2 and 2.35 that is 18.2, against the 17.4 that PE gives. Second, 15 was not the upper end of its own numbers: the pair in [rows 13] summed to 13.4, with the piece 15.8, and with these gaps it would already have read 18.1. Third, the collision with a slab load was taken for chance. In the new order low(2) sets off both, so the load and gather 0 are issued 0.35 us apart in most groups, and gather 0 is never among the quick ones; the median landing went from 5.1 to 9.1. Rival C had the right place and too large a size: 1.3 to 3.5 us, not 6.5, in 13 r=2 groups, and 4 to 6 us more than before, not 15, in the r=1 groups.
- **Gathers 2 and 3 behind low(5)**, priced at 0.6 in a group: 3.5 to 4.0 (with the start of the turn) ahead of rows(2) in six r=3 and r=4 groups, and 13 us more in all in the growing r=2 groups (27.7 against 14.7). The prologue, priced at 3, cost nothing in all.
- **Part 5, r=1 groups, +16**: they took 28, its lower bound 3 and its upper 45 held; 5 of each group's 9 us go with the queue.
- **Part 4, the hold**: the mechanism was right. DVE's fourth piece took 2.61 and ended 1.1 after GpSimd's. Its size in an r=2 group stayed out of sight only as long as the queue made PE late anyway; set free, it came out as up to 2.7 us ahead of c = 4, where part 2 had 1.2, and "PE stays the bound: no cost" was wrong there. Silu's 0.34 was 0.11 at a group's first product and 0.28 behind it, and its stage cost of 8 to 11 us was not foreseen.
- **Part 2, the early turn, -10**: 14 to 16 in the other direction beside the bank, 4 beside bank and silu. The 0.80 at matmul 18 was to go with an earlier turn; it came back ahead of the turns, 47 us of 57 ahead of the second one, which was priced at 0.55 a group and took 1.6 to 1.8.
- **Rival B** (no hold) falls with 1578 ns for a piece, **D** in the form in which it was put (GpSimd's op 0.85 longer): it is 2535 ns in the mean, 0.15 longer. **E** falls with the bank alone.
- **TensorE's clock** has no term in the sum: matmuls at the lower level cost 40 us of stage before and 47 after, and 4 to 8 of the bank's 62 us came from there (32 and 36 us with the bank alone).

The prediction's estimate from the Trainium skill (6377) leaned on gathers whose instruction grows beside DVE. The Trainium skill ("SBUF — State Buffer", section "SBUF: two separate sides") speaks of about 3100 ns for a DMA issued by GpSimd beside a DVE copy. Here the 78 gathers of the changed kernel took 974 ns in the mean (1146 before), with GpSimd's own pieces around them; what grew is the time to landing, and it grew beside slab loads. So no run here shows a wait of that size, and 6377 came from a cause that was not there.

## What to carry to other kernels

When work is put on a queue that also waits for transfers, add up everything from the last piece to the next, issue gaps included, and ask which event releases the neighbours: if the same event starts a large load, the transfer always meets it, and its median from the old order says nothing. A piece given to a second engine is only worth what the first engine can do meanwhile; count that before counting the share. And bundle fewer edits: the bank alone was worth 52 to 57 us, and the others together lost about 80.

## What the runs showed of the hardware

- A gather of 128 rows beside a 2 MB load lands late: of the 78 of the changed kernel, the 43 that were issued beside one took 7.8 to 11.5 us, the 35 others 4.0 to 4.7.
- The hold depends on where DVE's inputs are. Beside GpSimd's pieces in the changed kernel all 159 low pieces and 9 e_act (two SBUF inputs) ended 1.08 and 0.28 us after GpSimd's instruction; 57 e_aTl, 41 e_hTl and 9 e_tt, with one input in PSUM, kept their 0.42, 0.69 and 0.69 us.
- A clamp of one SBUF input (TENSOR_SCALAR 128x256) is held as well: e_gg takes 294 to 295 ns in the mean where GpSimd makes no pieces and 481 with the fourth piece on GpSimd, where 67 of them end 0.15 us after GpSimd's. 76 e_tt beside the same pieces stayed at 0.69 us.
- Before the change DVE stands idle between groups for 3.27 to 3.78 us after r = 3 or 4, and for 4.73 to 7.10 after r = 1 or 2, without exception. Nesting the branches did not change it. What it is stays open. It stands ahead of the waits for the first gated rows of 14 groups, 3.0 to 4.4 us each, which are the largest that are left.
